# Paged latent-attention decode: turning cached keys on VectorE in 32x32 blocks instead of on TensorE

## What is computed

```python
q_lat = jnp.einsum('bthe,rhe->bthr', q_nope, w_uk)
s_past = jnp.einsum('bthr,bsr->bths', q_lat, lat_past) + jnp.einsum('bthe,bse->bths', q_rope, kr_past)
s_new = jnp.einsum('bthr,bur->bthu', q_lat, ckv) + jnp.einsum('bthe,bue->bthu', q_rope, kr)
s_new = jnp.where(causal[:, None, :], s_new.astype(jnp.float32) * SOFTMAX_SCALE, -jnp.inf)
s = jnp.concatenate([s_past.astype(jnp.float32) * SOFTMAX_SCALE, s_new], axis=-1)
p = jax.nn.softmax(s, axis=-1).astype(h.dtype)
o_lat = (jnp.einsum('bths,bsr->bthr', p[..., :past], lat_past)
         + jnp.einsum('bthu,bur->bthr', p[..., past:], ckv))
o = jnp.einsum('bthr,rhe->bthe', o_lat, w_uv).reshape(B, T, N_HEADS * V_DIM)
return o @ w_o, ckv, kr
```

## Time and profile before

| what | us |
|---|---|
| device time, median of 3 runs (lowest, highest) | 1280.6 (1280.03, 1282.7) |
| device time of the profiled execution | 1281.81 |
| its span from first to last instruction | 1280.0 |
| PE busy in the span | 1232.1 (96%) |
| DVE busy | 667.5 (52%) |
| ACT busy | 526.4 (41%) |
| POOL busy | 131.4 (10%) |

### The profile page before, as it was taken

One profiled execution on the slowest core, in us unless ns is written; L12 is line 12 of the kernel. 1 busy time (PEld: TensorE's weight loads), 2 busy tenths in 40 slices (PEclk: granted clock), 3 DMA queues, 4 the chain that ended last, 5 costly groups with the idle time before them and its releaser, 6 DMA issues.

```text
span 1280.0 us, 23693 instructions
## 1 busy us (share of the span) xinstructions
PE 1232.1 (96%) x9979; PEld 1146.1 (90%) x9979; DVE 667.5 (52%) x986; ACT 526.4 (41%) x722; POOL 131.4 (10%) x124
## 2 busy tenths in 40 slices
PE   5899999999999999999999999999899899999997
PEld 2899999989998999999899999987677499999997
DVE  1644444556675445445545545558655356555453
ACT  1533333343434444333544433354544235554332
POOL 3000001210040000022000001310111040000031
PEclk9999999999999999999999999999999999999999
DMA  9777554568675774355678534584377373444442
GB/s 362 284 293 275 203 215 161 180 204 289 233 279 202 296 294 167 124 180 176 245 265 298 192 126 162 179 309 144 140 297 276 113 263 104 180 164 165 137 160 82
DMA packets 68711, 269.45 MB, mean 211 GB/s; under 512 B 4704, under 2 KB 5152, under 8 KB 54416
## 3 DMA queue, kind: packets, MB, share of 16 engines
q1 hardware_dynamic: 35664, 184.57, 40.3%
q10 hardware_dynamic: 29792, 59.09, 12.6%
q0 software_dynamic: 3168, 24.52, 5.2%
HBM read 266.55 MB, written 1.62 MB: 210 GB/s over the span
## 4 chain that ended last, share of the span: by engine, by line
PE 88%; DVE 4%; DMA 3%; ACT 2%; SPq 1%; issue 0%; ACTq 0%; POOL 0%; DVEq 0%; POOLq 0%
PE bank L1274 25%; PE bank L1275 25%; PE bank L1276 25%; PE bank L1320 4%; PE bank L1564 2%; DMA ada_early<-in_w_ada 1%; PE bank L1616 1%; PE bank L1577 1%; DMA kr_past<-in_cache_kr,rows 1%; PE bank L1341 1%; ACT w_hi L604 1%; DVE w_lo L825 1%; DMA stage<-in_w_ci 1%; PE bank L1485 1%; DMA stage<-in_w_uq 1%; PE bank L1481 1%
## 5 line engine op out<-in xcount | busy, mean ns | idle before, releaser
L825 DVE TENSOR_TENSOR w_lo<-stage,w_hi 128x2048 fp32r<-128x2048 f32 (+2 forms) x182 | 374.7, 2060 | 295.2 <-ACT w_hi L604 294.8
L1274 PE MATMUL bank<-h_hi,w_hi 128*128 128x288 f32 x1608 | 477.0, 297 | 2.5 <-DVE w_lo L825 1.5
L1276 PE MATMUL bank<-h_hi,w_lo 128*128 128x288 f32 x1608 | 475.6, 296 | 0.0
L1275 PE MATMUL bank<-h_lo,w_hi 128*128 128x288 f32 x1608 | 475.1, 295 | 0.0
L604 ACT CAST w_hi<-stage 128x2048 fp32r<-128x2048 f32 (+2 forms) x182 | 304.2, 1674 | 248.8 <-PE bank L1276 168.9
L1274 PEld LDWEIGHTS bank<-h_hi,w_hi 128*128 128x128 f32 x1608 | 302.3, 188 | 7.2 <-issue 3.7
L1275 PEld LDWEIGHTS bank<-h_lo,w_hi 128*128 128x128 f32 x1608 | 302.6, 188 | 0.0
L1276 PEld LDWEIGHTS bank<-h_hi,w_lo 128*128 128x128 f32 x1608 | 302.3, 188 | 0.0
L1275 PE MATMUL bank<-gu_lo,w_hi 128*128 128x288 f32 x768 | 226.6, 295 | 0.0
L1276 PE MATMUL bank<-gu_hi,w_lo 128*128 128x288 f32 x768 | 226.4, 295 | 0.0
L1274 PE MATMUL bank<-gu_hi,w_hi 128*128 128x288 f32 x768 | 225.3, 293 | 0.0
(11 more groups left out here) (233 smaller groups left out, 974.3 us busy)
## 6 DMA issues: line engine op xcount, KB each, us to landing
stage<-in_w_gu SPq DMA_DIRECT2D x88, 1024.0 KB, 4.9
stage_ada<-in_w_ada ACTq DMA_DIRECT2D x53, 1024.0 KB, 9.2
stage<-in_w_down SPq DMA_DIRECT2D x64, 704.0 KB, 4.0
stage<-in_w_ci SPq DMA_DIRECT2D x16, 768.0 KB, 4.4
stage_ada<-in_w_ada SPq DMA_DIRECT2D x9, 1024.0 KB, 10.4
ada_early<-in_w_ada SPq DMA_DIRECT2D x4, 1024.0 KB, 14.9
stage<-in_w_co SPq DMA_DIRECT2D x4, 1024.0 KB, 6.6
stage<-in_w_wo SPq DMA_DIRECT2D x4, 1024.0 KB, 5.2
```

Source lines behind the costliest of these rows:

```text
L825: nc.vector.tensor_tensor(w_lo[part][:, 0:cols], stage[st_][:, 0:cols], w_hi[part][:, 0:cols], ALU.subtract).then_inc(lo_ready, 1)
L1274: nc.tensor.matmul(out, hi, x_hi, start=start, stop=False)
L1275: nc.tensor.matmul(out, hi, x_lo, start=False, stop=False)
L1276: return nc.tensor.matmul(out, lo, x_hi, start=False, stop=stop)
```

## The change

- VectorE turns the keys, from the gathered buffer straight to SBUF, in blocks of 32x32: five transpositions of 128x1024 per sequence, the chunks, four of latents (64 of the 256 values each) and one of rotary keys. TensorE's turns and both sets of copies go. VectorE turns chunks 0 to 2 of sequence b + 1 ahead of the maximum of b, chunks 3 and 4 behind it.
- In a chunk a block's 32 values lie in 32 partitions, and the four row blocks of the partitions hold different keys. The queries are therefore repeated in all four row blocks, once for all sequences: ten products with `spread` on TensorE ahead of `s_new`, copied by ScalarE to `q_rep` and into two old buffers for the rotary ones (`q_rs_low`, `sq_now`).
- Scores are 160 products per sequence, each of 32 rows, 32 columns and 128 keys, one on each of the 16 tiles of the array, in four banks, `s_banks`, which are not doubled.
- Values(b - 1) follow scores(b) on TensorE. ScalarE, not VectorE, copies `p_past_t` and `p_new_t`.
- A fourth latent buffer, `lat[3]`, lies where `stage` is; sequence 3 uses it, gathered once the second unit of `wo` is split. The third and fourth unit of `wo` are loaded once values(3) are done. `LAT_OF` is the table of sequence to buffer.
- Rotary gathers have semaphores of their own. `q_rep` lies in `stage_ada`, the place of the tail's quarter 0; that quarter is now the last of four (`TAIL_ORDER`).

The diff, cut to its core; the score, value and loop parts of TensorE stand in the order rows below:

```diff
-TURNS = QUARTERS * RT + 2
+BLK = 32
+KEY_BLOCKS = (KVL + ROPE) // BLK
+CHUNKS = KEY_BLOCKS // 2
...
         ring_tail = [stage_ada] + [over(f"ada_tail{q}", [P, C_TILES, 2, 2 * P], at) for q, at in
-                                   ((1, 40960), (2, 49152), (3, 66304))]
+                                   ((1, 40960), (2, 49152), (3, 32768))]
         ada_early = [over(f"ada_early{q}", [P, C_TILES, 2, 2 * P], 8192 * q) for q in range(RING)]
 
         uk = over("uk", [P, RT, D], 0)
@@ -374,10 +378,14 @@
 
         mask_s = over("mask_s", [QS, NSEQ, TS], 90880)
         ckv_tok = over("ckv_tok", [P, KVL], 89856)
-        lat = [over(f"lat{n}", [P, GROUPS, KVL], (66304, 24576, 40960)[n]) for n in range(3)]
+        lat = [over(f"lat{n}", [P, GROUPS, KVL], (66304, 24576, 40960)[n]) for n in range(3)] + \
+            [nc.alloc_sbuf_tensor_at("lat3", [P, GROUPS, KVL], F32, offset=stage_at)]
         kr_past = [over(f"kr_past{n}", [P, GROUPS, ROPE], (82688, 62208)[n]) for n in range(2)]
-        lat_t = [over(f"lat_t{rt}", [P, QUARTERS, QG * P], 16384 * rt) for rt in range(RT)]
-        kr_t = nc.alloc_sbuf_tensor_at("kr_t", [P, 2, QG * P], F32, offset=spare_lo)
+        chunk = [over(f"chunk{c}", [P, GROUPS, 2, BLK], at) for c, at in enumerate((0, 4096, 16384, 20480))] + \
+            [nc.alloc_sbuf_tensor_at("chunk4", [P, GROUPS, 2, BLK], F32, offset=spare_lo)]
+        spread = nc.alloc_sbuf_tensor_at("spread", [P, P // BLK, P // BLK, BLK], F32, offset=spare_lo)
+        q_rep = nc.alloc_sbuf_tensor_at("q_rep", [P, KVL // BLK, NSEQ, QS], F32, offset=stage_ada_at)
+        q_rep_rope = [q_rs_low, sq_now[:, 0:NSEQ * QS].rearrange("p (b q) -> p b q", b=NSEQ)]
...
@@ -393,7 +401,10 @@
         o_sum = over("o_sum", [P, NSEQ // C_TILES, KVL], 28672)
         o_tok = over("o_tok", [P, H // C_TILES, VD], 30720)
 
-        bank = [ctx.enter_context(nc.psum_tensor(f"bank{n}", [P, 512], F32)) for n in range(8)]
+        s_banks = ctx.enter_context(nc.psum_tensor("s_banks", [P, P // BLK, 512], F32))
+        s_past = s_banks[:, :, 0:QG * BLK]
+        bank = [s_banks[:, n, :] for n in range(P // BLK)] + \
+            [ctx.enter_context(nc.psum_tensor(f"bank{n}", [P, 512], F32)) for n in range(P // BLK, 8)]
 
 
         loaded = [sem(f"loaded{s}") for s in range(STAGES)]
...
@@ -452,6 +465,9 @@
         N_WARM = 16
         MLA_BLOCK = 4
         LAG = 3
+        TAIL_ORDER = (1, 2, 3, 0)
+        LAT_OF = (0, 2, 1, 3, 0, 2, 1, 0)
+        LAST_OF = {b: max(c for c in range(b) if LAT_OF[c] == LAT_OF[b]) for b in range(4, NSEQ)}
         BY_ROOT = (slice(0, 1), slice(1, 2), slice(2, 3), slice(3, 5), slice(5, 7), slice(7, KT))
         FINAL = (slice(0, 3), slice(3, 6), slice(6, KT))
         SUM_BANK = {LATENT: 0, TAIL: 2}
@@ -501,6 +517,8 @@
                         continue
                     if not isinstance(st.u, int) or st.u >= STAGES:
                         sp.wait_ge(lo_ready, st.u - (STAGES - 1))
+                    if seg.name == "mla_out" and st.place == STAGES:
+                        sp.wait_ge(pv_done, LAT_OF.index(3) + 1)
                     src = a["w_" + st.kind]
                     src = src[st.place] if isinstance(st.place, int) else \
                         src[bass.ds(st.place, 1), :, :].rearrange("a p n -> (a p) n")
@@ -510,9 +528,9 @@
                         for q in range(RING):
                             sp.dma_start(by_run(ring[q]), quarter(2, q)).then_inc(ada_loaded[q], 16)
                 if seg.name == "mla_out":
-                    for q in range(RING):
+                    for q in TAIL_ORDER:
                         if q == 0:
-                            sp.wait_ge(o_psum, 2 * H)
+                            sp.wait_ge(chunk_used, CHUNKS * NSEQ)
                         else:
                             sp.wait_ge(pv_done, NSEQ - 1 if q == RING - 1 else NSEQ - 2)
                         sp.dma_start(by_run(ring_tail[q]), quarter(TAIL, q)).then_inc(ada_loaded[q], 16)
...
-                nc.gpsimd.indirect_dma_start(out=lat[b % 3][:].rearrange("p g r -> p (g r)"), out_offset=None,
-                                             in_=a["cache_lat"], in_offset=at).then_inc(lat_in[b % 3], 16)
+            def rows_of(b):
+                return bass.IndirectOffsetOnAxis(ap=rows[:, b:b + 1], axis=0)
+
+            def gather_lat(b):
+                nc.gpsimd.indirect_dma_start(out=lat[LAT_OF[b]][:].rearrange("p g r -> p (g r)"), out_offset=None,
+                                             in_=a["cache_lat"], in_offset=rows_of(b)).then_inc(lat_in[LAT_OF[b]], 16)
+
+            def gather_kr(b):
                 nc.gpsimd.indirect_dma_start(out=kr_past[b % 2][:].rearrange("p g r -> p (g r)"), out_offset=None,
-                                             in_=a["cache_kr"], in_offset=at).then_inc(lat_in[b % 3], 16)
+                                             in_=a["cache_kr"], in_offset=rows_of(b)).then_inc(kr_in[b % 2], 16)
 
             pool.wait_ge(rows_step, 2)
             pool.wait_ge(q_lat_ready, 2)
             pool.wait_ge(q_rope_ready, ROPE_BATCHES)
             pool.dma_start(mask_s[:], a["mask_s"]).then_inc(mask_in, 16)
-            gather(0)
+            gather_lat(0)
+            gather_kr(0)
+            pool.wait_ge(lo_ready, SEG["mla_out"].base + STAGES)
+            gather_lat(3)
             pool.wait_ge(o_ready, 2 * H)
-            gather(1)
+            gather_lat(1)
+            gather_kr(1)
+            gather_lat(2)
             for b in range(2, NSEQ):
-                if b >= 3:
-                    pool.wait_ge(pv_done, b - 2)
-                pool.wait_ge(turned, TURNS * (b - 1))
-                gather(b)
+                pool.wait_ge(chunk_ready, CHUNKS * (b - 1))
+                gather_kr(b)
+                if 4 <= b + 2 < NSEQ:
+                    pool.wait_ge(pv_done, LAST_OF[b + 2] + 1)
+                    gather_lat(b + 2)
             for n in range(MLA_BLOCK + 1, DEPTH * N_SUB + 1):
                 squares(n)
 
...
-                    dst = lat_t[k % RT][:, k // RT, :] if k < QUARTERS * RT else kr_t[:, k - QUARTERS * RT, :]
-                    nc.scalar.copy(dst, bank[(TURNS * b + k) % 4][:]).then_inc(even_copied, 1)
-
-            copy_even(0, range(0, TURNS, 2))
+            for n in range(KEY_BLOCKS // 2):
+                act.wait_ge(q_rep_psum, n + 1)
+                if n < RT * 2:
+                    nc.scalar.copy(q_rep[:, 2 * n:2 * n + 2].rearrange("p a b q -> p (a b q)"), bank[n][:])\
+                        .then_inc(q_rep_ready, 1)
+                else:
+                    for half in range(2):
+                        nc.scalar.copy(q_rep_rope[half][:], bank[n][:, NSEQ * QS * half:NSEQ * QS * (half + 1)]
+                                       .rearrange("p (b q) -> p b q", b=NSEQ)).then_inc(q_rep_ready, 1)
             act.wait_ge(new_ready, 1)
+
+            def part_out(b):
+                act.wait_ge(pv_done, b + 1)
+                nc.scalar.copy(o_part[:, b, :], bank[7][:, KVL * (b % 2):KVL * (b % 2 + 1)]).then_inc(o_part_ready, 1)
+
             for b in range(NSEQ):
-                if b + 1 < NSEQ:
-                    act.wait_ge(sc_psum, b + 1)
-                    copy_even(b + 1, (0,))
                 act.wait_ge(max_ready, b + 1)
-                if b:
-                    act.wait_ge(pp_psum, b)
-                nc.scalar.activation(p_past[:], bank[4 + b % 2][:], ACT.Exp, bias=neg_past[:, b:b + 1], scale=SCALE,
+                nc.scalar.activation(p_past[:].rearrange("p (j i n) -> p i j n", j=QG, i=P // BLK),
+                                     s_past.rearrange("p i (j n) -> p i j n", j=QG), ACT.Exp,
+                                     bias=neg_past[:, b:b + 1], scale=SCALE,
                                      accum_out=sum_past[:, b:b + 1]).then_inc(p_past_ready, 1)
                 nc.scalar.activation(p_new[0:QS], s_new[:, b, :], ACT.Exp, bias=neg_past[0:QS, b:b + 1], scale=SCALE,
                                      accum_out=new_sum[:, b:b + 1]).then_inc(p_past_ready, 1)
-                if b + 1 < NSEQ:
-                    copy_even(b + 1, range(2, TURNS, 2))
-                act.wait_ge(pv_done, b + 1)
-                nc.scalar.copy(o_part[:, b, :], bank[7][:, KVL * (b % 2):KVL * (b % 2 + 1)]).then_inc(o_part_ready, 1)
+                if b:
+                    part_out(b - 1)
+                act.wait_ge(pp_psum, b + 1)
+                nc.scalar.copy(p_past_t[:].rearrange("p g n -> p (g n)"), bank[4 + b % 2][:]).then_inc(pp_ready, 1)
+                nc.scalar.copy(p_new_t[0:TS], bank[6][0:TS, 0:QS]).then_inc(pp_ready, 1)
+            part_out(NSEQ - 1)
             act.wait_ge(w_dev_ready, 1)
             nc.scalar.activation(w_exp[:], w_exp[:], ACT.Exp).then_inc(w_exp_ready, 1)
             act.wait_ge(o_sum_psum, 1)
...
+            def score(b, c):
+
+                pe.wait_ge(chunk_ready, CHUNKS * b + c + 1)
+                for k in range(2):
+                    for t in range(QUARTERS):
```

(15 more changed lines are left out.)

156 lines of the change are left out of this document (67 added, 89 removed).

## The result

The changed kernel takes 1328.97 us (median of 4 runs, 1325.04 to 1330.06) against 1280.74 for the kernel before: a ratio of 1.0365, 95% interval 1.0353 to 1.0378. It is slower by 48 us, where 1278.0 was forecast, and the time lies outside the range given. The profiled execution took 1328.51 us, its span is 1326.7 (before 1281.81 and 1280.0).

What follows compares the result with a forecast made beforehand. TensorE bounded the loop; afterwards VectorE would, at 7.36 us a period instead of 9.98. Through the tail -4.5, plus clock +2.0, is -2.5: 1279.3 profiled from 1281.81, 1.2 above the median, so 1278.0; range 1266 to 1298.

Steps and rivals of the forecast that it cites:

- Start: Ahead of the decode loop: ten query-spreading products add 4.3 us, then eight transpositions and the maximum; sequence 0 ends +7.0 us.
- M(0): End of VectorE's `neg_past` for sequence 0, forecast at 944.9 us; M(b) is the same landmark for sequence b.
- Transposition: VectorE's 128x1024 key turn: 1225 ns, taken as 1.26 us with the gap between instructions, five per sequence.
- Scores: TensorE's 160 small products per sequence: sixteen tiles fully abreast, ten groups of 0.23 us, 2.33 us in all.
- the first rival: Tiles abreast only in part on TensorE: scores 3.5 us instead of 2.33, +3.5, 1281.5 us; chance 0.12.
- the 0.65: Scores per chunk on TensorE, in us: above this the forecast is wrong and the kernel not faster; 0.47 was expected.
- The two estimates that the prediction gives beside its sum: Scores per sequence from the skill page: 3.5 us by a tile gain of 10.6, 8.0 by 25 ns between starts.
- So VectorE sets the period, at 7.36: Decode loop: VectorE's five transpositions plus maximum, 7.36 us per sequence, exceed TensorE's path of 5.3; before, 9.98.
- Half clock: Rival: TensorE's idle time halves its clock in the loop, periods of 9.5 us, 1296 us in all; chance 0.13.
- The late gather: Rotary keys of sequence 6, queued on GpSimd behind latents of 7 that wait for values(4): VectorE stalls 7.9 us.
- Tail: After the loop: last adaLN quarter load 7.0 us after values(6), its product 1.0; `w_norm` turned at 1011.2, -4.5 us.
- the rival with two cycles an element: VectorE transpositions at two cycles an element: 12.7 us a sequence, M(6) 1031.6, +30, 1311 us; chance 0.06.

Runs made afterwards that it cites:

- new tokens first: Changed kernel with latents of b+1 gathered behind rotary keys of b, and new tokens' scores made ahead of the ten query-spreading products: 1326.06 us.
- two halves: Whole version of the changed kernel: 80 score products of 256 columns, sequences alternating partition halves, rotary keys gathered ahead, new tokens' scores first; 1278.96 us.
- late weights: The two halves version with sequence 7 in the fourth latent buffer, last two output-weight units loaded after all values, tail quarters into earlier-free buffers: 1269.37 us.
- wide: Changed kernel with 80 score products of 256 columns on two column groups instead of 160 of 128; half the scores left out: 1294.52 us.
- half: Changed kernel with 80 score products of 128 columns on two column groups, half the scores not computed: 1291.73 us.
- narrow before: Kernel before the change, each score product of 512 columns cut into eight of 64: 1300.36 us.
- halves narrow: The two halves version with all but the first eight of a sequence's 80 score products cut into two of 128 columns: 1309.55 us.

## Why the prediction was wrong

*Start: right in its number, for another reason in part.* M(0) came at 945.5 (944.9). VectorE's first transposition started where it was forecast. But taking away the 4.5 us ahead of it (new tokens first) gained 0.26 at M(0): TensorE sets it as well. VectorE had turned its eighth chunk at 943.1 and waited 1.33 us for scores of sequence 0, which took 7.04 us at half clock and had a gap of 1.99 in them. That the two came out within 0.6 us of the forecast is in part luck.

*Transposition: right.* 1225 ns measured, 1225 worked out from the earlier trace rows; to hit it to the nanosecond from forms of another operation is luck. Successive ones start 1.13 to 1.17 us apart, not 1.26, so VectorE needs 5 x 1.15 + 1.06 = 6.8 us per sequence, not 7.36.

*Scores: mis-sized, as in the first rival.* 208 records at full clock take 2.90 us:

```profile
989.40:992.30 2.90, 2.90 (x208) 2.61 (x206) 1.71 (x2) 0.65 (x2) 1.42 (x2) 1.00 0.60 158
```

At 13.9 ns a record, 320 of them are 4.5 us, not 2.33 and not 9.3: sixteen tiles run abreast in about half. That is 0.89 us a chunk, above the 0.65 that the text gave as a sign of being wrong. The first rival had 3.5. The two estimates that the prediction gives beside its sum, 3.5 and 8.0 us, lie on either side; the 25 ns from one start to the next, on which the second rests, are 13.9 here, and the measurement decides. By the forecast's own sum, TensorE's path per period would still have been 1.06 + 1.16 + 0.77 + 4.5 = 7.5, next to VectorE's 7.36, and the time some 6 us more; this doesn't make 1329.

*The step that failed is "So VectorE sets the period, at 7.36".* TensorE sets it, at 14.6. TensorE's side of the step, 5.3 us, was made up of array time and semaphores. That 720 instructions have to come to it in 7.36 us was not in the sum, nor in a rival. The number stood in the order rows and in the earlier trace rows: 640 records for scores where 212 had made a whole period. The text counted 320 records once, only to weigh the time between two starts. What the profile of before could not show was the price, since 212 in 9.98 us never ran short. The runs give it, as the sum of the gaps in the loop: at 212 no wait; at 400 in 7.3 to 7.9 us 0.7 to 1.8 us (two halves, late weights), and 5.0 and 3.2 (wide, half); at 548 in 10.8 us 12.0, most of it at the loop's two ends (narrow before); at 690 20.0 us (halves narrow); at 720 27.5 us.

The Trainium skill's page "Runtime: NRT & Kernel Launch", section "Instruction fetch mechanics", says that instructions are brought in blocks of 16 KB, 256 of them, ahead of their use, and that the cost is mostly hidden. The blocks are as in this trace (512, 256, 511, 767 records between gaps). That the cost is hidden holds for the kernel before and not for the changed one, where a block's end cost up to 4.6 us; the measurement decides.

*Half clock: a rival that came true in part, at the wrong place in the chain of causes.* It was given 1296 at 0.13. The clock did alternate, to 0.50 and back, but for the most part as a consequence: five of its seven falls came in gaps of 3.9 us or more, and in the whole versions of 400 instructions, where TensorE is busy nearly throughout, it stayed at 1.00 in nearly all windows of the loop. The fall at the start, ahead of any gap, is the rival's own. Five values in the changed kernel's loop, at 2.91, 3.57, 3.22, 3.01 and 3.50 us instead of 1.86, show what it costs there: 6.9 us. The scores of sequences 1 to 7 kept TensorE busy for 40.8 us, where 2240 records at 13.9 ns are 31.2: by this estimate another 9.6.

*The late gather: mechanism right, worth wrong.* VectorE's wait for the rotary keys was 12.1 us (7.9 forecast), at the place named. But the order of the gathers, to which the text put it down, was worth nothing: behind the rotary keys stood the latents of 7, as late as they. The forecast should have asked what is late next. An earlier buffer for these latents, together with the tail's loads, gained 9.6 us (1278.96 to 1269.37) once instructions were not short.

*Tail: mechanism right.* Values(6) end at 1050.49, the last quarter lands 8.81 us after its issue at 1050.91 (7.0 forecast), and its product takes 1.67 at half clock (1.0). With the loads moved this went from the path.

Put together from M(0) to M(7), where 45 us more than forecast were spent: 25.5 us of gaps between 945 and 1050, 16.5 us of values and scores at half clock, and some 7 x 2.2 = 15 us of scores beyond the forecast at full clock. They overlap with one another and with the time of VectorE that the forecast had in their place, so they need not add up to 45. How much of it the clock alone is was not separated: in no run of the changed kernel's 720 instructions did the clock stay up. What is shown is that the stops end with the landing of instruction blocks, that some 400 instructions instead of 720 give back 34 us in the changed kernel, and that cutting the products of the whole version small costs 31 us there, 18 of them in such stops.

Slips of the prediction's arithmetic decide nothing: 2.5 below 1280.6 is 1278.1, the gathers set 6.6 us a period in one place and 6.9 in another, and M(6) of the rival with two cycles an element is 1030.7 by the text's own terms, not 1031.6.

## What to carry to other kernels

Cutting a product into small tiles saves array time and multiplies instructions: count TensorE's records per microsecond, not only its columns, and compare with stretches of the same profile that run without "issue" gaps. Here some 50 a microsecond (400 in 7.9 us) ran nearly free when they were wanted evenly, and 90 (690 wanted in 7.5 us) did not. In none of these runs did two instruction packets start less than 3.24 us apart, which is 79 a microsecond at most (an estimate, 256 / 3.24). Where gaps come at multiples of 256 records and each ends shortly behind a packet of the instruction queue, wider products help even at equal array time. And before a late transfer is priced by the queue order ahead of it, look at when the next transfer in that queue lands.
